# Sixteen modulation chunks summed inside layer 0's attention instead of its mixing stage, in a two-layer diffusion backbone step

## The reference, cut to what matters

```python
def modulation(cvec, w_mod, b_mod):
    m = jax.nn.silu(cvec) @ w_mod + b_mod
    return tuple(t[:, None, :] for t in jnp.split(m, 6, axis=-1))

def trunk_layer(x, mod, ..., mixer):
    shift1, scale1, gate1, shift2, scale2, gate2 = mod
    h = rmsnorm(x, g_mix_pre) * (1 + scale1) + shift1
    y, ctx_state = mixer(h)
    x = x + gate1 * rmsnorm(y, g_mix_post)
    h = rmsnorm(x, g_ffn_pre) * (1 + scale2) + shift2
    x = x + gate2 * rmsnorm(conv_ffn(h, w_ffn_in, w_ffn_conv, w_ffn_out), g_ffn_post)
    return x, ctx_state
```

## Time and profile before

| what | value |
|---|---|
| median of three runs | 1804.48 us |
| the profiled execution | 1804.35 us |
| its span in the profile | 1802.6 us |
| TensorE busy | 1659.5 us, 92% |
| VectorE busy | 1092.2 us, 61% |
| ScalarE busy | 722.5 us, 40% |
| GpSimd busy | 114.5 us, 6% |
| a chunk's load, issue to landing (median of 26, 512 KB each) | 3.7 us |
| layer 0's attention | about 187 to 297 us of the span |
| layer 0's mixing stage | about 299 to 380 us of the span |

### The profile page before, as it was taken

The page is one execution under the profiler, slowest core; times in us unless marked ns, Lnnn a source line. Parts: engine busy times, 40 slices in busy tenths (PEclk is TensorE's granted clock), DMA queues, the critical chain, the costliest instruction groups (busy, mean ns, idle before and its releaser), DMA issues.

```text
span 1802.6 us, 33042 instructions
## 1 busy us (share of the span) xinstructions
PE 1659.5 (92%) x12288; PEld 1586.0 (88%) x12288; DVE 1092.2 (61%) x2046; ACT 722.5 (40%) x1186; POOL 114.5 (6%) x121
## 2 busy tenths in 40 slices
PE   5799899969999999999889979989799999999995
PEld 1799687959999999999889968779699999999995
DVE  4497676767777767777753248762566651466524
ACT  3722665226343134442241138652366541343410
POOL 1060210000000000000000032500000000000000
PEclk7899899979999999999999979999899999999998
DMA  8233001422434533345322110102012222222211
GB/s 295 89 110 124 31 2 48 157 77 72 118 113 142 199 116 114 105 145 193 120 79 81 48 62 2 45 1 62 32 59 71 80 81 72 70 71 80 92 49 59
DMA packets 42768, 160.63 MB, mean 89 GB/s; under 512 B 5072, under 2 KB 6096, under 8 KB 42304
## 3 DMA queue, kind: packets, MB, share of 16 engines
q1 hardware_dynamic: 39888, 152.00, 25.7%
q0 software_dynamic: 1584, 6.61, 1.1%
q10 hardware_dynamic: 1216, 0.92, 0.2%
HBM read 155.98 MB, written 3.54 MB: 88 GB/s over the span
## 4 chain that ended last, share of the span: by engine, by line
PE 79%; DVE 6%; issue 4%; ACT 2%; DMA 1%; DVEq 1%; ACTq 0%; SPq 0%
PE ps L1373 28%; PE ps L1374 28%; PE ps L1537 4%; PE ps L1566 4%; PE ps L1412 3%; PE ps L1552 3%; PE ps L1428 2%; PE ps L1486 1%; DMA ring<-in_wmodt 1%; DVE x L899 1%; PE ps L1487 1%; PE ps L1387 1%; PE ps L1386 1%; DVE ring L801 1%; DVE wlo L793 1%
## 5 line engine op out<-in xcount | busy, mean ns | idle before, releaser
L499 ACT ACTIVATE whi<-raw 128x1024 fp32r<-128x1024 f32 (+1 forms) x166 | 185.6, 1120 | 603.5 <-PE ps L1374 505.1
L1373 PE MATMUL ps<-hh,whi 128*128 128x320 f32 x920 | 286.7, 312 | 12.9 <-DVE wlo L793 12.9
L1373 PE MATMUL ps<-hl,whi 128*128 128x320 f32 x920 | 285.1, 310 | 0.0
L1373 PE MATMUL ps<-hh,wlo 128*128 128x320 f32 x920 | 285.1, 310 | 0.0
L1374 PE MATMUL ps<-hl,whi 128*128 128x320 f32 x920 | 285.0, 310 | 0.0
L1374 PE MATMUL ps<-hh,whi 128*128 128x320 f32 x920 | 284.9, 310 | 0.0
L1374 PE MATMUL ps<-hh,wlo 128*128 128x320 f32 x920 | 284.9, 310 | 0.0
L793 DVE TENSOR_TENSOR wlo<-raw,whi 128x1024 fp32r<-128x1024 f32 (+1 forms) x166 | 219.5, 1324 | 75.2 <-ACT whi L499 74.8
L1373 PEld LDWEIGHTS ps<-hh,whi 128*128 128x128 f32 x920 | 173.1, 188 | 14.5 <-DVE wlo L793 14.5
L1374 PEld LDWEIGHTS ps<-hh,whi 128*128 128x128 f32 x920 | 173.2, 188 | 0.0
L1374 PEld LDWEIGHTS ps<-hl,whi 128*128 128x128 f32 x920 | 173.2, 188 | 0.0
(11 more groups left out here) (209 smaller groups left out, 3322.1 us busy)
## 6 DMA issues: line engine op xcount, KB each, us to landing
raw<-in_w SPq DMA_DIRECT2D x134, 512.0 KB, 3.6
work<-in_wmodt SPq DMA_DIRECT2D x54, 512.0 KB, 3.6
raw<-in_w SPq DMA_DIRECT2D x32, 704.0 KB, 4.2
ring<-in_wmodt SPq DMA_DIRECT2D x26, 512.0 KB, 3.7
work<-in_wmod SPq DMA_DIRECT2D x16, 512.0 KB, 5.0
work<-in_rpb POOLq DMA_DIRECT2D x8, 480.0 KB, 4.3
x<-in_x SPq DMA_DIRECT2D x1, 2560.0 KB, 17.4
out_x<-x SPq DMA_DIRECT2D x8, 320.0 KB, 2.2
```

The source lines that it names most:

```text
L499: nc.scalar.activation(whi[:, s, 0:kk * P], raw[:, s, 0:kk * P], ACT.Copy).then_inc(s_hi, 1)
L1373: T.matmul(bankA[s], slot(w, s, k), h[:, k, 0:HT], start=st, stop=sp_)
```

## The change

Layer 0's attention gets chunks 10 to 25: one behind `take_values` of every second unit (units 1, 3, ..., 27), one behind unit 28 and one behind unit 29. The first product of a chunk goes to a free part of `work` (`product_att`). SP's queue loads chunks 12 to 25 ahead of its wait for the end of the attention, each as soon as the chunk two before it is summed. The mixing stage keeps no chunk and no chunk load.

```diff
--- before.py
+++ after.py
@@ -227,6 +227,7 @@
         erow = ring(0, 4, RPB)
         pts = work[:, 3968:5248].rearrange("p (s n) -> p s n", s=2)
         product0 = work[:, 4096:5120]
+        product_att = work[:, 0:1024]
         ring1 = [work[:, 2572:2572 + 1024], work[:, 3968:3968 + 1024]]
         mrow = [yf[0:4, i * 512:(i + 1) * 512] for i in range(2)]
 
@@ -414,17 +415,14 @@
                 chunk_in(m, m % 2, ring0)
             for s in range(2):
                 wide(14 + s, s, w8, 14 + s, 8)
+            for m in range(12, 26):
+                sp.wait_ge(s_mused, m - 1)
+                chunk_in(m, m % 2, ring0)
             sp.wait_ge(s_oe, 30)
             sp.dma_start(cwide1[:, :, :].rearrange("p a n -> p (a n)"), a["cwide"]).then_inc(s_cwide, 16)
-            sp.wait_ge(s_mused, 12)
-            for b in range(2):
-                chunk_in(12 + b, b, ring0)
             with sp.Fori(0, 3) as p:
                 for s in range(2):
                     wide(2 * p + (16 + s), s, w8, 2 * p + (16 + s), 8)
-                    sp.wait_ge(s_mused, 4 * p + (2 * s + 14))
-                    for b in range(2):
-                        chunk_in(4 * p + (2 * s + 14 + b), b, ring0)
             for n in (22, 23, 24):
                 wide(n, n % 2, w8, n, 8)
             sp.wait_ge(s_t, 24)
@@ -1078,6 +1076,9 @@
                         for job in units[i + 2]:
                             neg_max(job)
                     take_values(unit)
+                    if layer == 0 and (i % 2 or i == 28):
+                        m = 10 + i // 2 + (i > 28)
+                        mod_chunk(m, m % 2, (4 if m % 2 == 0 else 7) + (m - 10 + m % 2) // 2, ring0, cwide0, product_att)
 
             def prepare_attention(n, slots):
 
@@ -1155,10 +1156,6 @@
                         V.tensor_tensor(chunk(ffl, h), fft, chunk(ffh, h).bitcast(F32), ALU.subtract).then_inc(s_ffl, 1)
                 run((layer, f"fin{half}"), f, after if mods is not None else None)
 
-            def mods_mix(i, s):
-                for b in range(2):
-                    mod_chunk(2 * i + (2 * s + 12 + b), b, i + (s + (5, 9)[b]), ring0, cwide0, product0)
-
             def mods_fin(m0, n0):
                 return lambda h: mod_chunk(h + m0, 1, h + n0, ring1, cwide1, product1)
 
@@ -1189,7 +1186,7 @@
                     ffn_half(1, 1)
                     y_phase((1, "fout1"), True)
 
-            y_phase((0, "mix"), False, mods_mix)
+            y_phase((0, "mix"), False)
             finish_mod(26, 16, 40, 4, ((0, 1), (0, 2)))
             dve.wait_ge(s_coef, 6)
             post_norm(0, 1)
```

## The result

The changed kernel takes 1835.07 us (median of 4 runs, 1832.02 to 1835.38), the kernel before 1803.28 us in the same comparison. The ratio is 1.0177, 95% interval 1.0153 to 1.0200: slower by 1.8%, 4 us above the forecast of 1831 and inside its range. Against the kernel before of the same comparison the change is 31.8 us, where 26.8 had been forecast.

A forecast was written before the change was run, and what follows sets the result against it. TensorE, busy 92% of the span, was taken as the bound, with VectorE holding up layer 0's mixing stage. 26.6 + 2.6 + 8.5 - 10.9 = +26.8 us on 1804.35 gave 1831 us, range 1818 to 1848.

The forecast's parts named there:

- The gain: Layer 0's mixing stage without chunks takes as long as layer 1's, 76.73 instead of 87.63 us: 10.90 us gained.
- The places in the attention: Each of sixteen chunks delays the next `copy_turned` and so TensorE's `sum_values`; the attention becomes 26.6 us longer.
- GpSimd beside them: Chunks at units 1, 11, 7 and 17 overlap GpSimd's query work and run at half speed there: 2.6 us.
- t = 0, 1, 2, 3 and 4: Attention units a chunk stands behind; TensorE loses 1.29, 1.73, 1.14, 1.93 and 2.14 us per chunk respectively.
- the hand-off from `copy_turned` to `sum_values`: In the attention, `sum_values` starts 0.69 us after `copy_turned` starts for a latent block, 0.47 us for a context block.
- the doubling of the earlier trace: Half a chunk beside GpSimd's pooling took 2.31 us instead of 1.22; the forecast used this half speed in the attention.
- The clock: Ten new TensorE idle times in the attention could lower its clock; five falls of 1.7 us taken, 8.5 us.
- The rival without falls: TensorE's clock does not fall in the attention, so the kernel takes 1822.7 us; chance 27%.
- The rival of a clock that stays low: Each of ten clock falls lasts twice 3.4 us, costing 34 us at most: 1856.7 us; chance 12%.
- The other side: VectorE's idle room in the attention, 10.53 us in ten units, covers the chunks: 1797.8 us, faster; chance 4%.

The follow-up runs named there:

- E1: Changed kernel with chunks 10 to 25 in the attention summed over 8 of 1024 columns only, loads and waits kept; ratio 0.9940 to the kernel before, median 1789.01 us.
- E5: Changed kernel with four idle 128x128 matmuls on TensorE ahead of each `sum_values` that follows a chunk; ratio 1.0096 to the kernel before, median 1815.86 us.
- E4: Changed kernel with each whole chunk moved within its unit, behind invert and ahead of `neg_max`; ratio 1.0028 to the kernel before, median 1807.48 us.
- E3: Changed kernel with the same sums as half chunks, one behind every attention unit and two behind the last two; ratio 1.0022 to the kernel before, median 1804.15 us.
- E6: Changed kernel rearranged: twelve half chunks behind t = 0 and 2, three chunks before mixing, one behind each of seven mixing units; ratio 0.9934 to kernel before, 1792.06 us.

## Why the prediction was right, point by point

**The gain.** Forecast 10.90 us from the two layers' windows, measured 10.73, and the same in E1. Using layer 1 as the measure of layer 0 without chunks was the safest step of all.

**The places in the attention.** Forecast 26.6 us, and 2.6 for GpSimd beside them, 29.2 together; measured 24.3 (E5 less E1). The mechanism was right at each place: the idle times of TensorE behind t = 0, 1, 2, 3 and 4 were 1.01, 2.19, 1.15, 1.85 and 1.85 us where 1.3, 2.0 (and 3.1 with GpSimd), 1.1, 1.9 and 2.1 had been worked out. The term mis-sized is the hand-off from `copy_turned` to `sum_values`. I took 0.69 us for a latent block from the earlier trace rows; behind a chunk it is 0.47 to 0.48. Over the eleven chunks with a latent block behind them, that is 2.4 us too much.

The 0.69 us were read wrongly. For a latent block `sum_values` also waits for ScalarE's share of the turned probabilities, and without a chunk this is what ends last. ScalarE's copies, for the `sum_values` of 220.15 us in the kernel before and of 225.03 us in the changed one:

```profile
218.91 1.14 ACT L662 ACTIVATE work<-ps 128x512 f32<-128x512 f32 x2 [1.18 <-PE ps L1553]
```

```profile
223.79 1.14 ACT L660 ACTIVATE work<-ps 128x512 f32<-128x512 f32 x2 [2.25 <-PE ps L1550]
```

They end at 220.05 and 224.93 us, and both times `sum_values` starts 0.10 us later, while VectorE's copy has been done for 0.27 us. The profile names VectorE as the releaser all the same. Behind unit 5's chunk ScalarE is done at 219.93 us, VectorE's copy at 221.47, and `sum_values` starts at 221.53. No run changed ScalarE's copy to test this, but one at 293.82 us agrees too: it starts 0.69 us after VectorE's copy starts, and 0.10 us after ScalarE's ends.

GpSimd accounts for another 1.2 of the 4.9 us (next point). The last 1.3 us were not followed up.

**GpSimd.** Forecast 2.6 us, measured 1.45 us of VectorE's time. The four halves that met it took 1.66, 1.51, 1.65 and 1.51 us instead of 1.22. The first of them, then GpSimd's two conversions beside it, and the second of these in the kernel before, with no chunk beside it:

```profile
200.88 1.66 DVE L799 SCALAR_TENSOR_TENSOR ring<-ring,cwide 128x1024 f32<-128x1024 f32 x1
```

```profile
200.85 0.61 POOL L1265 CAST qh<-qk 128x512 fp32r<-128x512 f32 x1 [15.29 <-PE ps L1534]
...
201.40 1.29 POOL L1265 CAST qh<-qk 128x128 fp32r<-128x128 f32 x1
```

```profile
203.02 0.29 POOL L1268 CAST qh<-qk 128x128 fp32r<-128x128 f32 x1
```

The half was 0.44 us longer than alone, and GpSimd's first conversion ran on beside it for 0.58 us. The second one took 1.29 us instead of 0.29 and ended at 202.69 us, right behind the half (202.54). The two did not slow each other evenly: each looks held up by one instruction of the other. That fits the Trainium skill's rule ("SBUF — State Buffer", "Who interferes with whom"), by which contention for the ports that VectorE and GpSimd share is an exclusive lock. What the prediction made of the rule, a half that waits for all of GpSimd's 2.5 us, did not happen; nor did the doubling of the earlier trace rows over the whole overlap. These are readings of a trace; no run was made to test them.

**The clock.** Forecast five falls and 8.5 us, measured seven falls and 11.05 us. Five was the middle between "none" and "ten" and not worked out, so that it came near was luck; the price of a fall, 1.7 us, was sound (11.05 / 7 = 1.6). The rival without falls (1822.7 us) is refuted for this kernel: at idle times of 1.75 to 2.19 us, seven of nine brought a fall. The rule of thumb in the Trainium skill ("TensorE: Matmul & The Clock Gate", "HAM oscillation"), by which only gaps longer than any of these harm, does not hold here: E4's falls came after 1.41 and 1.69 us, and E5 shows by its 11 us that it matters. The rival of a clock that stays low did not occur: each stretch ended after 3.4 us, but for the one into the mixing stage, which was 6.8 us long.

**The rest.** 3.1 us outside the stages touched had not been foreseen. Since a part of it is one more low stretch in unchanged code, and since the start of the program alone moved by 6.9 us among these profiles (first scores at 184.59 us in the kernel before, at 177.69 in E5), it may not belong to the change.

**The other side.** That VectorE's idle time covers the chunks was given 4%. E3 shows what of it is true: the same sums cost a third when cut to pieces nearer the slack, or half if the falls of the clock are left out (11.9 against 24.3 us). E6 shows where it is fully true: 1.15 us behind t = 0 and t = 2.

The errors went both ways: -4.9 us in the places, +2.5 in the clock, +0.2 in the gain not had, and 2.8 in the other stretches. So it was luck that 1831 lies within 1 us of the profiled execution (1832.02): the terms were off by up to 4.9 us and cancelled.

## What to carry to other kernels

An engine's idle share says little of what can be put beside it. Ask how long its idle time is in one piece at the place where the work shall stand, and who waits for the instruction behind it; then cut the work to that size. And where TensorE is made to wait in pieces of two microseconds, count the falls of its clock as well as the waits: here they were 11 of the 35 us that the attention lost. When two engines prepare the input of a third, look at both for the one that ends last; the releaser that the profile names may be the other.

## What the runs showed of the hardware

- TensorE's granted clock fell to 1.2 GHz after idle times of only 1.75 to 2.19 us in the changed kernel, seven times out of nine, and in E4 after 1.41 and 1.69 us, two times out of five. Idle times of 0.25 to 1.15 us in the changed kernel never did. Seven low stretches of the changed kernel's attention lasted 3.4 us each, the eighth, into the mixing stage, 6.8 us. What tells the idle times with a fall from those without stays open.
- Four idle matmuls, about 1 us together, in each of 15 gaps kept the clock at 2.4 GHz from 193 to 315 us and made the attention 11 us shorter. Work whose result nobody reads paid for itself, though E3, E4 and E6, which leave fewer or shorter idle times, are faster than this version.
- After a wait for VectorE's copy of 0.42 us, TensorE began 0.05 to 0.06 us after the copy's end, and 0.10 us after the end of ScalarE's copy where that one came last.
- A sum of VectorE over 128x1024 took 1.22 us alone and 1.66 us beside GpSimd's conversions, while one of these took 1.29 us instead of 0.29.
